# Two layers with product-key experts on one core: choosing the first tile earlier, asking the queries of heads 2 to 5 one by one

## The reference, cut to what matters

```
q = (hb @ peer_wq).reshape(128, 8 heads, 2, 128)          # queries of a block of 128 tokens
s = einsum("thsd,hskd->thsk", q, peer_keys)               # scores against 128 keys per side
s_top, i_top = top_k(s, 16)                               # per side
cand = s_top[:, :, 0, :, None] + s_top[:, :, 1, None, :]  # 256 candidate pairs
g_score, c_idx = top_k(cand, 16)                          # 16 experts of 16384
gates = softmax(g_score)
act = gelu(einsum("thkd,td->thk", u[experts], hb)) * gates
y = einsum("thk,thkd->td", act, v[experts])
```

## Time and profile before

| | |
|---|---|
| median of three runs | 4521.0 us (4516.7 to 4523.3) |
| the profiled execution | 4527.9 us, span 4526.1 us |
| mean granted TensorE clock | 0.831 of full speed |
| busy: TensorE, VectorE, Pool, ScalarE | 68%, 63%, 33%, 24% of the span |
| DMA, mean over the span | 329 GB/s; the gathers take 71.7% of 16 engines' span |
| gathers | 1280, from 782.4 to 4493.8 us |

### The profile page before, as it was taken

The page is one execution under the profiler, slowest core; times in us unless marked ns, Lnnn a source line. Parts: engine busy times, 40 slices in busy tenths (PEclk is TensorE's granted clock), DMA queues, the critical chain, the costliest instruction groups (busy, mean ns, idle before and its releaser), DMA issues. The chain is left out here.

```text
span 4526.1 us, 38384 instructions
## 1 busy us (share of the span) xinstructions
PE 3097.1 (68%) x12512; PEld 1370.6 (30%) x12512; DVE 2871.1 (63%) x6909; ACT 1085.6 (24%) x2958; POOL 1491.7 (33%) x1384
## 2 busy tenths in 40 slices
PE   7999979555665565655566565999766665555555
PEld 3645545322222222221222122565422222111111
DVE  1524745777778778775555554664788888555554
ACT  2121222222222222221122211463322222111111
POOL 0001300343443443444344442000344444444443
PEclk9999989787887887777788877999888777777777
DMA  4113731999999999999999996101999999999998
GB/s 167 39 38 124 251 127 58 420 420 415 411 418 414 412 416 410 415 414 422 419 420 421 419 421 283 38 1 37 381 419 420 413 414 405 422 422 421 422 421 348
DMA packets 229660, 1488.59 MB, mean 329 GB/s; under 512 B 25932, under 2 KB 31532, under 8 KB 59220
## 3 DMA queue, kind: packets, MB, share of 16 engines
q0 software_dynamic: 184320, 1342.26, 71.7%
q1 hardware_dynamic: 43764, 139.82, 8.5%
q10 hardware_dynamic: 1376, 4.06, 0.2%
HBM read 1483.76 MB, written 2.28 MB: 328 GB/s over the span
## 5 line engine op out<-in xcount | busy, mean ns | idle before, releaser
L1671 PE MATMUL banks<-arena 128*64 128x512 f32 x5120 | 1604.2, 787 | 1322.3 <-ACT arena L1812 1245.2
L1531 POOL DMA_INDIRECT arena<-experts,arena x1280 | 1419.8, 1109 | 2484.1 <-PE banks L1671 1601.0
L1947 DVE CUSTOM_DVE_ANT_0 arena<-arena 128x1024 f32<-128x1024 f32 x1280 | 1544.1, 1224 | 931.2 <-DMA arena<-experts,arena 912.0
L1671 PEld LDWEIGHTS banks<-arena 128*64 128x64 f32 x5120 | 445.8, 180 | 2389.7 <-ACT arena L1812 1398.1
L1804 ACT ACTIVATE arena<-arena 128x4 f32<-128x4 f32 x320 | 66.1, 206 | 2017.2 <-DVE arena L1947 1993.2
L1812 ACT ACTIVATE arena<-arena 128x64 f32<-128x64 f32 x1280 | 339.4, 335 | 28.3 <-DVE arena L1935 0.4
L1594 PE MATMUL banks<-arena 128*128 128x128 f32 (+2 forms) x1280 | 296.3, 386 | 4.7 <-DMA arena<-wq 2.9
L1594 PEld LDWEIGHTS banks<-arena 128*128 128x128 f32 x1280 | 205.5, 194 | 90.1 <-issue 22.1
L427 PE MATMUL banks<-arena 128*128 128x512 f32 (+1 forms) x640 | 210.3, 488 | 1.8 <-PEq L201 1.8
L1545 PE MATMUL banks<-arena 128*128 128x512 f32 x416 | 183.9, 599 | 2.3 <-PEq L891 1.5
L427 PEld LDWEIGHTS banks<-arena 128*128 128x128 f32 x640 | 121.2, 191 | 87.3 <-issue 79.7
(11 more groups left out here) (240 smaller groups left out, 3133.5 us busy)
## 6 DMA issues: line engine op xcount, KB each, us to landing
arena<-l_w_ada SPq DMA_DIRECT2D x48, 1024.0 KB, 4.9
arena<-wq SPq DMA_DIRECT2D x80, 512.0 KB
arena<-experts,arena POOLq DMA_INDIRECT x1280
arena<-l_w_in SPq DMA_DIRECT2D x7, 2048.0 KB, 8.9
arena<-l_w_out SPq DMA_DIRECT2D x4, 1536.0 KB, 12.7
arena<-keys SPq DMA_DIRECT2D x40, 128.0 KB
arena<-l_w_o SPq DMA_DIRECT2D x4, 1024.0 KB, 8.4
arena<-gates SPq DMA_DIRECT2D x6, 512.0 KB, 6.5
```

What stands on the lines that cost most here:

```text
L1531: pool.indirect_dma_start(slots[u % NS], None, tbl, bass.IndirectOffsetOnAxis(ap=expert[:, c % RING, k:k + 1], axis=0)).then_inc(land[u % ...
L1671: mm = pe.matmul(core["ps"][QS * j:QS * j + QS, c, :], diag[:, g % 2, k, :], v[:, D + c * 512:D + (c + 1) * 512], start=(g % (NB * PH) == ...
L1947: dve.tensor_tensor_reduce(u, u, rep[i // PH % 2][:, k % NQ, :], 1.0, 0.0, ALU.mult, ALU.add, dots[:, k:k + 1]).then_inc(dot["sem"], up(dot))
```

## The change

Layer by layer, the order in which the engines' lists are written changes, and which of it lies ahead of the first position; what is computed stays.

- Two choices are made ahead of the positions in both layers (`EARLY = 2`, before 4 and 2), and six events count as asked ahead (`AHEAD = 6`, before 6 and 4), but only events 0 and 1 really are. Queries and scores of events 2 to 5 stand behind the weighted sums of positions 0 to 3, one event each, and on ScalarE their four copies (`answer(e)`) stand behind the diagonals of the same position. Later events: from positions 5, 8, 11 in layer 0 (events 6 to 8) and 4, 6, 8 in layer 1.
- Ahead of the positions, tile 0's query follows its columns with four projection instructions in between, and its scores after two more; choice 0 stands on VectorE ahead of gate_out(1, 1), choice 1 around gate_out(2, 1). The two row spreads of tile 0 stand apart.
- VectorE issues dot_batch(0) and (1) ahead of the last tile's norm_rows, turn_rows of that tile stands behind weighted sum 0, and ScalarE's low_columns behind the copies of event 2. In layer 1 gate_identity(0) and dot_batch(0) stand ahead of gate_out of the last tile, and ScalarE issues diagonals(0) ahead of that tile's squares.
- The gate for the expert mixer has a semaphore of its own (`g2l`), so gate_out waits for the output gates alone.

```diff
-    EARLY = tiles - 2
+    EARLY, AHEAD = 2, 6
...
-    for e in range(tiles, E):
-        query_at[e] = max(chosen_at[first[e], 0] - 5, query_at.get(e - 1, -2) + 2)
+    for e in range(AHEAD, E):
+        query_at[e] = max(chosen_at[first[e], 0] - 5, query_at.get(e - 1, AHEAD - EARLY - 2) + 2)
...
-            sp.dma_start(g2, gate_rows(core, layer, 1, 0)).then_inc(gr["sem"], up(gr, 16))
+            sp.dma_start(g2, gate_rows(core, layer, 1, 0)).then_inc(g2l["sem"], up(g2l, 16))
...
@@ tensor
-            for t in range(tiles + 2):
-                if t < tiles:
-                    project(t, 0)
-                if t >= 2:
-                    scores(t - 2, 0)
-                    scores(t - 2, 1)
-                if 1 <= t <= tiles:
-                    turn_rows(t - 1)
-                if t < tiles:
-                    project(t, 1)
-                if 1 <= t <= tiles:
-                    query(t - 1, 0)
-                    query(t - 1, 1)
-                if t == 1:
-                    for j in range(NQ):
-                        spread_rows(0, j)
-                if 2 <= t < tiles:
-                    spread_choice(t - 2)
+            project(0, 0)
+            project(0, 1)
+            project(1, 0)
+            turn_rows(0)
+            project(1, 1, 0, 2)
+            query(0, 0)
+            query(0, 1)
+            project(1, 1, 2, 3)
+            scores(0, 0)
+            scores(0, 1)
+            project(1, 1, 3, K)
+            spread_rows(0, 0)
+            project(2, 0, 0, K // 2)
+            spread_rows(0, 1)
+            spread_choice(0)
+            project(2, 0, K // 2, K)
+            turn_rows(1)
+            project(2, 1, 0, 2)
+            query(1, 0)
+            query(1, 1)
+            project(2, 1, 2, 3)
+            scores(1, 0)
+            scores(1, 1)
+            project(2, 1, 3, K)
+            for t in range(3, tiles):
+                project(t, 0)
+                turn_rows(t - 1)
+                if t == 3:
+                    spread_choice(1)
+                project(t, 1)
...
+                if g + EARLY < AHEAD:
+                    for side in range(2):
+                        query(g + EARLY, side)
+                    for side in range(2):
+                        scores(g + EARLY, side)
+                if g == 0:
+                    turn_rows(tiles - 1)
@@ scalar
+            def answer(e):
+                for side in range(2):
+                    query_out(e, side)
+                for side in range(2):
+                    scores_out(e, side)
+
+            squares(0)
+            root(0)
+            low_columns(0)
+            answer(0)
+            rows_spread(0, 0)
+            softmax(0)
+            rows_spread(0, 1)
+            squares(1)
+            root(1)
+            low_columns(1)
+            answer(1)
+            softmax(1)
...
+            for t in range(2, tiles):
+                if layer == 1 and t == tiles - 1:
+                    diagonals(0)
+                squares(t)
+                root(t)
+                if t < tiles - 1:
+                    low_columns(t)
+            for g in range(POS):
+                if layer == 0 or g:
+                    diagonals(g)
+                if g + EARLY < AHEAD:
+                    answer(g + EARLY)
+                if g == 0:
+                    low_columns(tiles - 1)
+                if half_at(g) and half_at(g)[1] == 0:
+                    softmax(half_at(g)[0])
@@ vector
-            dve.wait_ge(gr["sem"], at(gr, 16 * conds + 16))
+            dve.wait_ge(gr["sem"], at(gr, 16 * conds))
+            gate_out(0, 0)
+            gate_out(0, 1)
+            norm_rows(0)
+            gate_out(1, 0)
+            high_columns(0)
+            choose_a(0)
+            choose_b(0)
+            gate_out(1, 1)
+            choice_out(0)
+            norm_rows(1)
+            gate_out(2, 0)
+            high_columns(1)
+            choose_a(1)
+            gate_out(2, 1)
+            choose_b(1)
+            for t in range(3, tiles):
+                norm_rows(t - 1)
+                if layer == 0:
+                    gate_out(t, 0)
+                high_columns(t - 1)
+                if t == 3:
+                    choice_out(1)
+                if layer == 1:
+                    gate_identity(0)
+                    dot_batch(0)
+                    gate_out(t, 0)
+                gate_out(t, 1)
+            if layer == 0:
+                gate_identity(0)
             for g in range(POS):
-                dot_batch(g)
+                if layer == 0 and g == 0:
+                    dot_batch(0)
+                if g != 1:
+                    dot_batch(g if g else 1)
+                if g == 0:
+                    norm_rows(tiles - 1)
...
+                if g == 0:
+                    high_columns(tiles - 1)
```

More of the change, by code:

```diff
@@ L1505, in _ @@
                 sp.wait_ge(rd["sem"], at(rd, TL))
-                sp.dma_start(g2, gate_rows(core, layer, 1, 1)).then_inc(gr["sem"], up(gr, 16))
+                sp.dma_start(g2, gate_rows(core, layer, 1, 1)).then_inc(g2l["sem"], up(g2l, 16))
                 sp.wait_ge(free["sem"], at(free, steps * TOPK))
@@ L1541, in project @@
                     pe.wait_ge(oad["sem"], at(oad, 2 * (t - 1) + c + 1))
-                for k in range(K):
+                for k in range(k0, k1):
                     if t == 0 and k == K // 2:
@@ L1781, in prepare, with diagonals @@
                     i.then_inc(plo["sem"], up(plo))
[L1783 to L1800, removed]
+            def answer(e):
[15 more added lines that the diff above has]
+            softmax(1)
+            def diagonals(g):
                 i, b = g // NB, g % NB
@@ L1951, in add_tile @@
                 dve.wait_ge(free["sem"], at(free, PH * TOPK * (t + 1)))
-                if t == TL:
-                    dve.wait_ge(gr["sem"], at(gr, 16 * conds + 32))
+                dve.wait_ge(g2l["sem"], at(g2l, 16 if t < TL else 32))
                 dve.tensor_tensor(pair(core, 0), pair(core, 0), g2, ALU.mult).then_inc(xup["sem"], up(xup))
@@ L1995, in prepare @@
                                           ALU.mult).then_inc(plw["sem"], up(plw))
-            dve.wait_ge(gr["sem"], at(gr, 16 * conds + 16))
[L1998 to L2001, removed]
-                    gate_out(t, 0)
-                if t >= 1:
-                    high_columns(t - 1)
-                if 2 <= t < tiles:
-                    choose_a(t - 2)
-                    choose_b(t - 2)
-                if t < tiles:
-                    gate_out(t, 1)
-                if 2 <= t < tiles:
-                    choice_out(t - 2)
-            gate_identity(0)
-            for g in range(POS):
-                dot_batch(g)
+            dve.wait_ge(gr["sem"], at(gr, 16 * conds))
[17 more added lines that the diff above has]
+                if layer == 0:
+                    gate_out(t, 0)
+                high_columns(t - 1)
[8 more added lines that the diff above has]
+                gate_identity(0)
+            for g in range(POS):
+                if layer == 0 and g == 0:
[4 more added lines that the diff above has]
+                    norm_rows(tiles - 1)
                 if half_at(g - 1) and half_at(g - 1)[1] == 1:
```

10 lines of the change are left out of this document (5 added, 5 removed).

## The result

The changed kernel takes **4531.9 us** (median of 14 runs, 4526.9 to 4534.3), the kernel before, in the same job, 4523.3 us (14 runs, 4516.7 to 4527.4). The ratio is 1.0018, 95% interval 1.0011 to 1.0026: about 8 us slower (5 to 12). The forecast was 4517.0, 4 us faster, with 4503 to 4531 as its range. The time lies just above that, close to 4531, the place of rival 2 at half its size.

The account below looks back on a forecast made before the run. Both expert phases were taken as bound by the gathers. Layer 0: -11.7 + 8.4 + 11.5 - 1.5 = +6.7; layer 1: -17.4 + 5.6 + 5.3 - 4.0 = -10.5; sum -3.8, from 4521.0 to 4517 us, range 4503 to 4531.

Parts of the forecast that it names:

- rival 2: Positions 0 to 3, both layers: late query weights make sums 4 to 5 us later at three positions; 4539, likelier 4531; 17%.
- First gathers: Start of each layer: first gather issued 8.6 us earlier in layer 0 (773.8), 16.2 earlier in layer 1 (3151.4).
- Sums 0 to 2: First weighted sums start at 802.1, 821.5, 833.5 in layer 0 and 3186.7, 3204.6, 3217.0 in layer 1.
- Position 2 to 3: Step between weighted sums 2 and 3: two table loads, a row spread, a late second wq half of 11.9 us; 17 us.
- 25th gather: Layer 1: lands at 3242.6 against 3239.1, part of the 5.3 us lost to gaps there.
- Bytes given back: Query weights and keys no longer loaded before the first landing: 8.4 us in layer 0, 5.6 in layer 1.
- first landing: Layer 0's first gather lands at 780.1 against 791.8, 11.7 us earlier.
- Ends of tiles: Layer 0: choices two behind instead of four are covered by two positions of about 10 us, so cost nothing.
- rival 3: Layer 0: choices two behind run late at tile boundaries, Pool waits for VectorE a few us each; 4525; 7%.
- The refill of layer 1: Layer 1: 4 us lost before over the refill behind the empty queue and not now, a guess; -4.0.
- The square root of the last tile: Layer 0, ScalarE: stands ahead of diagonals(0), waits for 8 landings; first sum at 802.1, only 5.5 us earlier.
- Rival 4: Table switches in positions 0 to 3, both layers: a drain of about 1.38 us each, some 10 us; 4525; 3%.

Follow-up runs that it names:

- e4: e2 with the six query-weight loads of heads 3 to 5 made into unread space, their queries using head 2's weights: 4516.5 us, 0.9976 of the kernel before.
- e1: New order in layer 0 alone, layer 1 as in the kernel before: 4537.5 us, 1.0026 of the kernel before.
- e9: e1 with gelu and diagonals of sum 1 ahead of the first softmax on ScalarE: 4531.9 us, 1.0016 of the kernel before.
- e10: e9 with VectorE's norm_rows of the last tile ahead of the dots of batch 1: 4520.7 us, 0.9991 of the kernel before.
- e2: New order in layer 1 alone, layer 0 as in the kernel before: 4522.7 us, 0.9995 of the kernel before.
- e5: e2 with query weights of heads 3 and 4 staged after the last projection, head 5's behind head 2's query: 4511.1 us, 0.9969 of the kernel before.
- e3: e2 without the six query-weight loads of heads 3 to 5, their queries using head 2's weights: 4515.1 us, 0.9974 of the kernel before.
- e8: e1 without the query-weight loads of heads 3 to 5, their queries using head 2's weights: 4533.0 us, 1.0017 of the kernel before.
- e7: e2 with the edits of e5 and e6 and the last tile's norm ahead of dot_batch(1): 4508.8 us, 0.9962 of the kernel before.
- e6: e2 with gelu and diagonals of sum 1 ahead of the first softmax on ScalarE: 4516.0 us, 0.9979 of the kernel before.

## Why the prediction was wrong

**First gathers: right.** Layer 0's at 772.9 (said 773.8), layer 1's at 3151.4 after the shift (said 3151.4). The last projections, the eight early gathers and the 13th's issue (3189.9 shifted, said 3189.7) came as walked.

**Sums 0 to 2: right.** Layer 0: 801.2, 820.3, 833.0 against 802.1, 821.5, 833.5. Layer 1, shifted: 3185.5, 3202.9, 3215.7 against 3186.7, 3204.6, 3217.0. ScalarE waited for VectorE's choice between sums 0 and 1, as it was to show.

**Position 2 to 3: the step that failed.** The prediction's "such a half took 11.9 us: 17" was the size of this position. It took 22.5 us in layer 0 and 23.3 in layer 1, and sum 3 was 4.4 and 4.8 us later than said. Two things were too small. The late half took 14.1 and 15.2 us from issue to landing, behind the first half and the keys (401 GB/s from 829 to 853). And TensorE, which had stood idle for that half (5.2 us in layer 0), was then granted the lower of its two clock levels, 1.2 GHz; two windows of the changed kernel:

```profile
844.35:848.13 3.78, 3.78 (x17) 3.78 (x18) 3.71 (x11) 0.00 (x0) 0.00 (x0) 0.50 1.00 405
...
852.27:855.50 3.23, 3.23 (x32) 3.23 (x34) 3.19 (x7) 2.43 (x6) 0.00 (x0) 0.54 0.69 284
```

The first is the half query, 3.78 us where the half ahead of it took 2.05 at 1.00; the second is the row spread, 3.2 us to the start of sum 3 where the one ahead of sum 2 took 1.8. That is about 3 of the 4.4 us. The walk of the prediction reckoned with the low clock in the weighted sums alone; only its upper bound had it in the queries. From sum 0 to sum 4 the chain took 65.4 and 64.3 us, where it had 58 to 61.

In layer 1 that one wait widened the gap behind sum 3 to 5.6 us (the prediction's 25th gather, 3.5 late), and e4, which takes the wait away and keeps the bytes, is 6 to 9 us faster (the low clock goes with the wait, so the two aren't priced apart). This is rival 2's mechanism, at one position of each layer and not at three; I had weighed it at 17%. The 11.9 us of the earlier trace rows is no odd case, it is close to the median of 12.1 above; the loads of this one position were the slow ones.

**Bytes given back: right in layer 0, too dear beside gaps.** I charged every moved byte at 420 GB/s, 8.4 and 5.6 us. All of layer 0's gathers can be counted: from 784 to 2790 the kernel before moves 831.71 MB in 2006 us, from 774 to 2800 the changed one 834.43 MB in 2026 us, which begins 10 us sooner and ends 10 later. The 2.7 MB more are 6.5 us at 420 GB/s, so 13.5 of the 20 us are time without bytes, about the 14.7 of the gaps less what the kernel before lost there. The prediction had 8.4 and 10.0 (11.5 - 1.5) for the two: the bytes were about right, the gaps too small. How full the DMA is from 2 us behind the first gather on, over 100 us, goes with the times: in layer 0 412 GB/s before, 345 in the changed kernel, 346 in e1, 374 in e9, 413 in e10; in layer 1 378 before, 341 in the changed kernel, 326 in e2, 354 in e4, 372 in e5. Where there are gaps, taking bytes away gives less than their price: e3 and e4 put 1 to 3 us on 3.1 MB, and e8 has 332 GB/s in place of e1's 346.

The first landing itself was 13.3 us sooner (first dot at 778.51, below, against 791.81), said 11.7.

```profile
778.51 1.23 DVE L1984 CUSTOM_DVE_ANT_0 arena<-arena 128x1024 f32<-128x1024 f32 x1 [5.98 <-DMA arena<-experts,arena]
```

**Ends of tiles: at nothing, and in the balance nothing.** The two windows above lose 8.5 us, 2.1 before, and rival 3's sign, lost time beyond position 5, is there. But from 900 to 2700 the changed kernel moves as much as the one before, so this isn't part of the 8 us. e10 still loses 3.7 + 4.2 us at these places (108 GB/s in 1492 to 1497, 128 in 1828 to 1834) and is faster than before. Whether the choices two ahead make these two gaps stays open: no kernel with four ahead and the new start was tried.

**The refill of layer 1: a guess, about half borne out.** I let 4 us go with the old empty queue. Its refill ran at 250 and 374 GB/s (3212 to 3224, 3.1 us lost), the new one at 383 (3197 to 3207, 0.9 lost). The empty queue itself only moved: because just eight gathers go early, the new order has one of its own, 3187 to 3197 at 58 GB/s, in the place of the old one at 3208. The gap behind sum 3 and the refill explain some 4 of the 8 us by which layer 1 missed; the rest stays open.

**The square root of the last tile: seen and left there.** The prediction says that it waits "behind dot_batch(1), 8 landings", and so starts the first sum only 5.5 us early. It was taken as a fact of the schedule. With e9's order around it, e10 shows that these two lines are worth 11 us: the positions form a chain of 58 us from sum 0 to sum 4 (58.5 in e9, 57.5 in e10) against the prediction's 51 of landings, so whoever starts it 10 us sooner ends it ahead of the DMA. In layer 1 the diagonals of sum 0 already stand ahead of that root, and sum 0 stays where it was in e7; that the edit by itself gives nothing there isn't shown, since e7 has e6's edit too.

**The table loads** took 1.28 us with the next instruction 0.01 us behind; ScalarE ahead of sum 0 in the changed kernel:

```profile
798.47 1.28 ACT L1826 ACT_TABLE_LOAD   x1
799.76 0.21 ACT L1826 ACTIVATE arena<-arena 128x4 f32<-128x4 f32 x1
```

Rival 4, a drain behind every switch, is wrong here: the rule of the Trainium skill, "ScalarE: Activation LUTs", section "What ACT_TABLE_LOAD costs", is not borne out at this switch. But a switch of tables in the chain still costs its 1.28 us twice where an exponential is put between two Gelus, and that was part of what e6 and e9 took out.

## What to carry to other kernels

When work is moved from an idle prologue between the first steps of a full pipeline, its arithmetic is the small part: write down the serial chain from step to step, with the requests for data that each step now makes one step ahead, and compare it with what the steps have to feed. Give every load in that chain a space of its own and ask for it before the pipeline fills; two free strips and two reorderings of a line or two turned 8 us lost into 18 won. And look first at what stands ahead of the first step in each engine's queue: an early start of a serial chain is kept by all of it.

## What the runs showed of the hardware

A 512 KB load beside a full gather queue is far from its bandwidth: 1.2 us at 420 GB/s, but a median of 8.0 us from issue to landing over the kernel, 12.1 from 800 to 870, and 14.1 and 15.2 us when asked behind another half and the keys. The keys, a quarter of its size, take 11.2 us over the kernel, so it isn't the size that one pays for; that it is the place in the queue is my reading. The Trainium skill, "DMA: Bandwidth & Descriptors", section "Queues, rings and completion order", says that each DMA engine takes turns between its queues packet by packet. With the page's 1342.26 MB in 184320 packets for the gathers and 139.82 MB in 43764 for the loads, 7.3 and 3.2 KB each, turns would give the loads 30% of 420 GB/s, and half, keys and half (1.18 MB) 9 us, an estimate that takes the profile's packets for those of that section; the trace shows 14.1, and no run here isolates it.

The same six loads moved in the busy phase (e4 against e3) cost 1 to 3 us where their bytes at 420 GB/s are 7.5: a phase that has gaps takes extra bytes at less than their price (not told from nothing, and the interval reaches to about 7).

A wait of TensorE costs more than its length: behind 5.2 us without work the next half query ran at a granted clock of 0.50 and took 3.78 us in place of 2.05, and the spread behind it 3.2 in place of 1.8 (changed kernel, layer 0; layer 1 shows the same, 0.51 and 0.55).
